# First modulation of a transformer block: column slabs by feature halves, and the first projections in two halves

## The reference, cut to what matters

```python
mod_x = silu(c) @ w_ada + b_ada          # [6 * 1024]; the same for the context with c_ctx
sh1, sc1, gt1, sh2, sc2, gt2 = split(mod_x, 6)
h  = rms_norm(x,   g_attn) * (1 + sc1)  + sh1      # [256, 1024]
hc = rms_norm(ctx, g_attn) * (1 + csc1) + csh1     # [256, 1024]
qa, ka, va, qb, kb, vb = split_projection(h  @ w_qkv)   # widths 512, 128, 128, 512, 512, 512
_,  ka_c, va_c, _, kb_c, vb_c = split_projection(hc @ w_qkv)
# attention, w_o, a mixture of 32 experts, then a retention layer, a gated FFN, an S5 layer, a second FFN
```

## Time and profile before

| | |
|---|---|
| median of the runs | 2076.93 us |
| the profiled execution: its own time | 2072.86 us |
| its span | 2071.0 us |
| TensorE busy | 1957.9 us (95%) |
| VectorE, ScalarE, GpSimd busy | 633.0, 392.8, 201.5 us |
| chain of work that ended last | TensorE 69%, DMA 21%, VectorE 5% |
| loaded from HBM | 613.20 MB, mean 297 GB/s |

### The profile page before, as it was taken

How to read it: one execution, slowest core, us unless ns; L and a number is a source line. 1 busy time by engine, 2 the same in 40 slices (tenths; PEclk the granted TensorE clock), 3 DMA queues, 4 the chain that set the end, 5 groups by cost and what they waited for, 6 DMA issues and landing times.

```text
span 2071.0 us, 24426 instructions
## 1 busy us (share of the span) xinstructions
PE 1957.9 (95%) x9814; PEld 1235.9 (60%) x9814; DVE 633.0 (31%) x1401; ACT 392.8 (19%) x759; POOL 201.5 (10%) x274
## 2 busy tenths in 40 slices
PE   7999999998989998899999899999999999999998
PEld 4645654433333443333334376688888889888887
DVE  3767342213212222112122246331104216210421
ACT  3126211111111101101111021220113215320210
POOL 0000000000000000000000000010755932200000
PEclk9999999999999999999999999999999999999999
DMA  9986699999999999999999995834343342634330
GB/s 372 366 305 246 261 371 416 426 422 428 427 429 428 428 428 428 428 429 428 429 428 428 418 354 206 324 119 142 122 163 123 140 166 99 229 134 150 112 112 21
DMA packets 118928, 615.40 MB, mean 297 GB/s; under 512 B 5216, under 2 KB 9440, under 8 KB 90432
## 3 DMA queue, kind: packets, MB, share of 16 engines
q1 hardware_dynamic: 117088, 604.43, 73.0%
q0 software_dynamic: 1760, 9.83, 1.2%
HBM read 613.20 MB, written 1.05 MB: 297 GB/s over the span
## 4 chain that ended last, share of the span: by engine, by line
PE 69%; DMA 21%; DVE 5%; ACT 2%; issue 1%; SPq 1%; POOL 1%; DVEq 0%; ACTq 0%; POOLq 0%
PE psum L1057 32%; DMA ring<-in_w_in_dram 20%; PE psum L1413 19%; PE psum L1068 3%; PE psum L1377 2%; PE psum L1388 2%; DMA arena<-in_cT_dram 2%; PE psum L1299 1%; PE psum L1562 1%; PE psum L1172 1%; PE psum L1748 1%; PE psum L1104 1%; PE psum L1434 1%; PE psum L1200 1%; SPq L915 1%
## 5 line engine op out<-in xcount | busy, mean ns | idle before, releaser
L1413 PE MATMUL psum<-ring,arena 128*64 128x512 f32 (+1 forms) x3200 | 684.3, 601 | 68.5 <-DMA ring<-in_w_in_dram 67.2
L1057 PE MATMUL psum<-arena,ring 128*128 128x256 f32 (+1 forms) x3072 | 680.4, 384 | 2.1 <-ACT arena L1835 1.4
L1057 PEld LDWEIGHTS psum<-arena,ring 128*128 128x128 f32 x3072 | 581.7, 190 | 99.0 <-issue 18.8
L1413 PEld LDWEIGHTS psum<-ring,arena 128*64 128x64 f32 (+1 forms) x3200 | 222.4, 135 | 504.1 <-issue 434.5
L1968 ACT ACTIVATE arena<-psum 128x512 f32<-128x512 f32 (+1 forms) x144 | 79.0, 571 | 733.6 <-PE psum L1413 726.3
L2548 DVE TENSOR_SCALAR arena<-consts,arena 128x64 f32<-128x64 f32 (+2 forms) x64 | 15.7, 310 | 318.2 <-PE psum L1413 318.2
L2869 DVE SCALAR_TENSOR_TENSOR consts<-psum,smalls,consts 128x255 f32<-128x255 f32 (+1 forms) x88 | 38.4, 478 | 229.8 <-ACT consts L2113 229.0
L2573 DVE TENSOR_TENSOR arena<-psum,arena 128x512 f32<-128x512 f32 x60 | 38.6, 684 | 215.0 <-PE psum L1434 215.0
L2530 DVE SCALAR_TENSOR_TENSOR x<-psum,mod,x 128x256 f32<-128x256 f32 x128 | 55.6, 479 | 145.4 <-PE psum L1388 145.4
L3041 POOL DMA_DIRECT2D arena<-in_pos_dram x1 | 0.5, 543 | 909.0 <-PE psum L1541 909.0
L1388 PE MATMUL psum<-arena 128*128 128x256 f32 (+1 forms) x272 | 69.2, 399 | 3.8 <-issue 2.0
(11 more groups left out here) (397 smaller groups left out, 1656.9 us busy)
## 6 DMA issues: line engine op xcount, KB each, us to landing
ring<-in_w_in_dram SPq DMA_DIRECT2D x124, 2048.0 KB, 17.2
ring<-in_w_out_dram SPq DMA_DIRECT2D x64, 2048.0 KB, 17.2
ring<-in_w_ada_dram SPq DMA_DIRECT2D x36, 2048.0 KB, 13.7
ring<-in_w_up_dram SPq DMA_DIRECT2D x22, 2048.0 KB, 7.9
ring<-in_w_ret_dram SPq DMA_DIRECT2D x12, 2048.0 KB, 16.4
ring<-in_w_down_dram SPq DMA_DIRECT2D x16, 1408.0 KB, 5.9
ring<-in_w_qkv_dram SPq DMA_DIRECT2D x4, 2048.0 KB, 20.0
ring<-in_w_rout_dram SPq DMA_DIRECT2D x4, 2048.0 KB, 9.5
```

The source lines that it names most:

```text
L1057: ins = nc.tensor.matmul(bank(c)[:, at:at + n], w[:, k, m * P:m * P + P], r, start=(k == 0), stop=(k == k_tiles - 1))
L1413: ins = nc.tensor.matmul(psum[at:at + size, p, :], act[:, k, n:n + size], w, start=(k < 3 - halves), stop=(k >= KD - 3 + halves))
```

## The change

The modulation slabs 0 to 3 become column slabs of 512 columns by all 1024 rows, like the others (rows of 2 KB), in the order 0, 2, 1, 3: slab 0 is the shift of tiles 0 to 3, slab 2 their scale, 1 and 3 the same of tiles 4 to 7. The load order is ada0, ada2, qa, (context), kva, ada1, ada3, (small inputs), ada4, ada5, qb, ada6, ada7, kb, (constants), and from there as before. TensorE does half the products of qa, keys and values as soon as tiles 0 to 3 are ready, the other half later, into the same PSUM banks.

```diff
-MOD_KEYS = ([("ada", s) for s in range(12)] + ...
+MOD_KEYS = ([("ada", s) for s in (0, 2, 1, 3, *range(4, 12))] + ...
-GROUP_END = [4, 8, 12, 16, 19, 24, 26, 32, 36]
+GROUP_END = [2, 4, 12, 16, 19, 24, 26, 32, 36]
@@ plan
-    for key in MOD_KEYS[:4]:
+    for key in (*MOD_KEYS[:2], "qa", "kva", *MOD_KEYS[2:4]):
         slab(key, 0)
     chunk(("cols", 0))
-    chunk(("qa", 0), ("norm", 0), ("qa", 1))
-    slabs["qa"] = len(chunks)
+    take_turns(0, 5)
+    chunk(("norm", 0), ("cols", 1))
+    take_turns(2, 3, 1, 0)
+    slab("qa", 2)
     slab("kva", 2)
@@ source
-            if kind == "ada" and s < FIRST_ROWS:
-                return w_ada[T * s:T * s + T, 0:4 * BANK].rearrange("(k p) n -> p k n", p=P)
@@ SyncE
-                if n == 4:
+                if n == 2:
                     sp.dma_start(ctx_x, ...)
@@ TensorE
-            for key in MOD_KEYS[:4]:
+            for key in MOD_KEYS[:2]:
                 modulation_rows(key)
-                keep_busy({1: 6, 2: 6, 3: 1}.get(key[1], 0))
+                keep_busy(6 if key == MOD_KEYS[0] else 2)
             modulation_cols(0)
-            keep_busy(2)
-            (qa with norm(0) inside, keys, values)
+            keep_busy(4)
+            qa_half(0, half_k, 0)          # 16 matmuls of 128x256, tiles 0 to 3
+            norm(0)
+            key_half(1, 0, half_k)         # x tokens, tiles 0 to 3: 4 matmuls of 128x256
+            value_half(1, 0, half_k)       # x tokens: 8 of 128x128
+            modulation_rows(MOD_KEYS[2])   # ada1
+            pe.wait_ge(h_ready, KD)
+            key_half(0, 0, half_k)         # context tokens
+            modulation_rows(MOD_KEYS[3])   # ada3
+            value_half(0, 0, half_k)
+            modulation_cols(1)
+            qa_half(half_k, KD, KD)        # tiles 4 to 7
+            key_half(1, half_k, KD)
+            pe.wait_ge(h_ready, 2 * KD)
+            end(key_half(0, half_k, KD))
+            value_half(1, half_k, KD)
+            end(value_half(0, half_k, KD))
             features("qb", lambda k: h_all[:, k, T:N_KEYS], 2)
@@ ScalarE
-            scale_and_shift(1)
+            scale_and_shift(1, 0, KD // 2)
             norm(0)
             ...
-            scale_and_shift(0)
+            scale_and_shift(0, 0, KD // 2)
+            copy_rows(1)
+            scale_and_shift(1, KD // 2)
+            scale_and_shift(0, KD // 2)
@@ VectorE
-            modulation(0), then aff over 8 tiles (two instructions)
+            first_affine(0)                # bias, then aff of tiles 0 to 3
             add_squares(0)
             norm(0)
+            first_affine(1)                # bias, then aff of tiles 4 to 7
```

More of the change, by code:

```diff
@@ L162 @@
 BIAS_STEP = 13
-MOD_KEYS = ([("ada", s) for s in range(12)] + [("ada2", 0, s) for s in range(12)]
+MOD_KEYS = ([("ada", s) for s in (0, 2, 1, 3, *range(4, 12))] + [("ada2", 0, s) for s in range(12)]
             + [("ada2", 1, s) for s in (0, 1, 2, 3, 4, 5, 10, 11, 6, 7, 8, 9)])
 MOD_NUMBER = {key: n for n, key in enumerate(MOD_KEYS)}
-GROUP_END = [4, 8, 12, 16, 19, 24, 26, 32, 36]
-ROWS_BANK = [4, None, 7, 0, 1, 7, 5, 4, 6]
+GROUP_END = [2, 4, 12, 16, 19, 24, 26, 32, 36]
+ROWS_BANK = [4, 6, 7, 0, 1, 7, 5, 4, 6]
 GAP_KEYS = MOD_KEYS[19:24]
@@ L172 @@
 SUMMED_1 = 8
-FIRST_ROWS = 4
 def group_of(key):
@@ L886, in norm_turn @@
             return NORM_ORDER.index(i)
-        AFFINE = {0: 1, 1: 1, 2: 2, 3: 3, 5: 3, 6: 4, 7: 5}
+        AFFINE = {0: 2, 1: 2, 2: 3, 3: 4, 5: 4, 6: 5, 7: 6}
         def summed_in(n):
@@ L895, in rows_copy @@
         def rows_copy(group):
-            return max(group, 1)
+            return group + 1
         def rows_of(group):
@@ L1092, in modulation_rows @@
                 w = slab(key)
[L1093 to L1100, removed]
                 for k in range(KD):
@@ L1134, in _ @@
             pe.wait_ge(cond_ready, 2)
-            for key in MOD_KEYS[:4]:
+            for key in MOD_KEYS[:2]:
                 modulation_rows(key)
-                keep_busy({1: 6, 2: 6, 3: 1}.get(key[1], 0))
+                keep_busy(6 if key == MOD_KEYS[0] else 2)
             modulation_cols(0)
-            keep_busy(2)
-            features("qa", lambda k: h_all[:, k, T:N_KEYS], 2, first=h_tiles(1), within=lambda: norm(0))
-            pe.wait_ge(h_ready, 16)
-            arrived("kva")
@@ L1144, in _, with room, qa_half @@
-            w = slab("kva")
+            keep_busy(4)
+            def room(key):
+                if USE[key]:
+                    pe.wait_ge(acc_free[BANK_OF[key]], USE[key])
+            def qa_half(k0, k1, first):
+                w = slab("qa")
+                for m in range(4):
+                    for k in range(k0, k1):
+                        if m == 0:
+                            pe.wait_ge(h_ready, first + k - k0 + 1)
+                        ins = nc.tensor.matmul(half(("qa", m // 2), m % 2), w[:, k, m * P:m * P + P],
+                                               h_all[:, k, T:N_KEYS], start=(k == 0 and m % 2 == 0),
+                                               stop=(k == KD - 1 and m % 2 == 1))
+                    if k1 == KD and m % 2:
+                        end(ins)
@@ new lines, in key_half, with value_half @@
+            def key_half(a, k0, k1):
+                w = slab("kva")
+                for k in range(k0, k1):
+                    ins = nc.tensor.matmul(half(("kva", 0), a), w[:, k, 0:P], h_all[:, k, T * a:T * a + T],
+                                           start=(k == 0 and a == 1), stop=(k == KD - 1 and a == 0))
+                return ins
+            def value_half(a, k0, k1):
+                w = slab("kva")
+                for t in (2 * a, 2 * a + 1):
+                    for k in range(k0, k1):
+                        ins = nc.tensor.matmul(bank(("kva", 1))[:, t * P:t * P + P],
+                                               h_all[:, k, t * P:t * P + P], w[:, k, P:2 * P],
+                                               start=(k == 0 and t == 2), stop=(k == KD - 1 and t == 1))
+                return ins
@@ new lines, in _ @@
+            half_k = KD // 2
+            arrived("qa")
+            room(("qa", 0))
+            room(("qa", 1))
+            qa_half(0, half_k, 0)
+            norm(0)
+            arrived("kva")
+            room(("kva", 0))
+            key_half(1, 0, half_k)
+            room(("kva", 1))
+            value_half(1, 0, half_k)
[4 more added lines that the diff above has]
+            value_half(0, 0, half_k)
@@ L1145, in _ @@
+            modulation_cols(1)
+            begin(("qa", 0))
+            begin(("qa", 1))
+            qa_half(half_k, KD, KD)
             begin(("kva", 0))
[L1146 to L1149, removed]
+            key_half(1, half_k, KD)
+            pe.wait_ge(h_ready, 2 * KD)
+            end(key_half(0, half_k, KD))
             begin(("kva", 1))
[L1151 to L1155, removed]
@@ L1156, in _ @@
-            end(ins)
+            value_half(1, half_k, KD)
+            end(value_half(0, half_k, KD))
             features("qb", lambda k: h_all[:, k, T:N_KEYS], 2)
@@ L1827, in apply, with scale_and_shift @@
                 scale_and_shift(i)
-            def scale_and_shift(i):
+            def scale_and_shift(i, k0=0, k1=KD):
                 _, out, row, shift = NORMS[i]
-                act.wait_ge(affine_ready, AFFINE[i])
-                for k in range(KD):
+                act.wait_ge(affine_ready, AFFINE[i] if k1 == KD else 1)
+                for k in range(k0, k1):
                     act.wait_ge(normed_ready, 4 * norm_turn(i) + k // 2 + 1)
@@ L1844, in copy_rows @@
                     act.wait_ge(q_ready, 9)
-                elif group < 6 and group:
+                elif 1 < group < 6:
                     read_ready(act, ("cols", group - 2))
@@ L2268, in modulation @@
                 read_ready(dve, key)
-                at = 16 * (group % 3)
                 if group == 2:
@@ L2274, in modulation @@
                     ins = V.tensor_tensor(out, src, b, ALU.add)
[L2275 to L2279, removed]
+                elif group < 2:
+                    src = bank(key)[:, 0:32].rearrange("p (m n) -> p m n", n=8)[:, :, 0:4]
+                    src = src.rearrange("p m (s c) -> p s m c", c=2)
+                    out = mod[:, 0:16, :].rearrange("p (s h m) c -> p s h m c", s=2, h=2)[:, :, group]
+                    b = sml("b_ada")[:, 0:16].rearrange("p (s h m) -> p s h m", s=2, h=2)[:, :, group]
+                    ins = V.tensor_tensor(out, src, b.unsqueeze(3).to_broadcast([P, 2, 4, 2]), ALU.add)
                 else:
@@ L2294, in _, with first_affine @@
             norm(1)
[L2295 to L2302, removed]
+            def first_affine(group):
+                modulation(group)
+                copied(dve, ("cols", group))
+                dve.wait_ge(dve_step, own.n)
+                tiles, scales = slice(4 * group, 4 * group + 4), slice(8 + 4 * group, 12 + 4 * group)
```

(7 more changed lines are left out.)

## The result

The changed kernel took 2082.63 us (median of 7 runs, 2075.97 to 2085.15) against 2076.43 us for the kernel before (7 runs, 2071.28 to 2077.8). The ratio is 1.0035, with a 95% interval of 1.0023 to 1.0046: about 7.2 us slower (4.8 to 9.6). The profiled execution took 2075.97 us, span 2074.2 us.

What follows compares the result with a forecast made beforehand. Up to 100 us TensorE and the transfer queue were taken to bound the kernel. A 3.3 us later kb start plus 1.5 us of clock fall gave +4.8 us, 2081.7 us against the median; range 2076 to 2085.5.

Steps and rivals of the forecast that it cites:

- Keys and values end at 61.8 (60.9 to 62.4): Early products, set by ada3 landing at 41.2: keys and values end 1.8 us earlier than before (1.2 to 2.7).
- qb is issued when qa is complete and starts 0.9 us after the values: Load of qb waits for qa's slot: issued 54.7, lands 62.7 after 8.0 us from an empty queue.
- Three slabs behind the values instead of one: Before kb, ada6, ada7 and kb must land after the values: 18.8 us instead of 10.2, while qb covers 13.9.
- kb starts at 80.7, +3.3 us: TensorE stalls 4.1 us for kb's slab, so kb starts at 80.7 instead of 77.4; bounds +2.4 to +3.9.
- late by 1.4 us: Before the change, one slab between the rows products of ada2 and ada3 came late for a reason outside its bytes.
- The clock falls, 1.5 us: After TensorE idles about 4 us before kb, the clock drops to the 1.2 GHz level; 0 to 1.7 us, taken 1.5.
- Nothing else behind kb: After kb, vb's slack shrinks to 1.2 us and head norm refinement is 0.4 us late; cost 0, at most 0.4.
- The shift reaches the end whole: Behind vb, loads TensorE needs are issued when it frees slots, so the whole shift was carried to the end.
- Rival C: Not slower: stall absorbed behind kb, in the experts' stream; 0 us, 2076.9 or a little under; chance 0.10.
- Sum: Whole kernel: 3.3 for kb's later start plus 1.5 for the clock, +4.8 us, 2081.7 against the median.
- rival E: A third term: vb's slack gone too or the clock low twice as long; +7 to +8, 2084 to 2085; chance 0.09.
- Rival D (faster): Gain at the values kept, if kb lands by 75.9 or values end at 58.5; 2074 to 2075; chance 0.06.

Runs made afterwards that it cites:

- exchanging the slots: Changed kernel with ring slots of slabs 2 to 5 exchanged, so only kb waits for the values; 2071.29 us against 2073.79 for the kernel before, ratio 0.9985.
- the kernel with coupled slots: Kernel before with only the slot assignment edited, so ada6, ada7 and kb are all issued behind the values; 2081.17 us against 2073.79, ratio 1.0030.
- the kernel kept busy: Changed kernel plus 10 unread matmuls of 128x256 between qb and kb; 2078.81 us against 2073.79 for the kernel before, ratio 1.0019.
- the column slabs alone: Kernel before with column instead of row slabs for ada0 to ada3, in the old order; 2074.13 us against 2073.79, ratio 1.0000.
- The delay alone: Kernel before plus 17 unread matmuls of 128x256 between kb and the head norms; 2082.44 us against 2074.52, ratio 1.0037.

## Why the prediction was right, point by point

- *Keys and values end at 61.8 (60.9 to 62.4).* 62.04 in the profile. ada3 was awaited until 41.72 (41.2 predicted), and the second half of qa began at 47.65 (47.2), behind the 1.2 us for bias, vectors and ScalarE's first tile that the text had there.
- *qb is issued when qa is complete and starts 0.9 us after the values.* Issued at 55.03, started at 62.83, 0.80 us of waiting.
- *Three slabs behind the values instead of one.* Shown in the changed kernel, removed by exchanging the slots, and reproduced in the kernel before.
- *kb starts at 80.7, +3.3 us.* It started at 82.28, +4.9. This term was too small by 1.6 us: from the end of the values to kb's first matmul were 20.2 us, not 18.9. VectorE found ada6 landed at 69.89, as 62.06 + 8.0 would have it, and the two slabs behind it took 12.3 us and not the 10.8 of 2 x 5.42. In the kernel with coupled slots, where kb was awaited just so, they took 10.8 us (71.33 to 82.12):

```profile
69.89 0.48 DVE L2298 TENSOR_SCALAR arena<-ring,cond 128x512 f32<-128x512 f32 x1 [9.32 <-DMA ring<-in_w_ada_dram]
```
```profile
71.33 0.49 DVE L2263 TENSOR_SCALAR arena<-ring,cond 128x512 f32<-128x512 f32 x1 [11.88 <-DMA ring<-in_w_ada_dram]
```

So the 18.8 us that the prediction added up came true there, and what the changed kernel had beyond it is one slab, kb itself, late by 1.2 to 1.5 us in its two profiles and in that of the kernel kept busy. It is of the size of the "late by 1.4 us" between ada2 and ada3, which the prediction left out here. The rate did not fall: from 69.9 to 82.23 us 4.80 MB moved, at 391 GB/s, where two slabs have 4.19, which suggests that bytes of later loads went ahead of kb's last ones. In these three profiles one transfer of the instruction queue lies between the landings of ada7 and kb, and in the coupled kernel none; but with the slots exchanged one lies there too, if only 0.3 us before kb landed, and kb was not late (10.9 us behind ada6). The cause is open.
- *The clock falls, 1.5 us.* It fell, and cost 2.7 (30.29 - 27.5; and 2.7 by the kernel kept busy). Rows 8 had a low stretch of 3.4 us; here the low level held 6.8 us, of which 5.2 lay in kb, so the term was sized from the wrong example. It was also a weaker example than the text took it for. The same gap in front of the last attention products stands in all nine profiles, and a low clock followed it in two, the kernel before and the column slabs alone; the products behind it took 3.62 us in the kernel before and 1.97 in the changed one:

```profile
210.29 3.62 PE L1239 MATMUL psum<-arena 128*128 128x256 f32 x8 [0.78 <-ACT arena L1916]
```
```profile
219.21 1.97 PE L1277 MATMUL psum<-arena 128*128 128x256 f32 x8 [0.78 <-ACT arena L1957]
```

That the fall would come at kb was therefore not shown by that row; the runs show it. The rule of "TensorE: Matmul & The Clock Gate", Part 1, of the Trainium skill, that an idle engine is put at 1.2 GHz, agrees with the fall at 80.6 us and with its absence in the kernel kept busy.
- *Nothing else behind kb.* The +7.6 us of the head norms is found again at the first attention scores (150.2 against 142.6) and, less 0.4, in front of the output projection (221.0 against 213.8).
- *The shift reaches the end whole.* The delay alone shows it to within 2.5 us. Rival C, the stall absorbed down to nothing, is out, by this and by the +7.2 us at the end.
- *Sum.* +4.8 us forecast, +7.2 (4.8 to 9.6) measured. That the time itself came within 0.9 us of the forecast 2081.7 is partly luck: the median of before, from which it was counted, was 0.5 us lower in the seven runs than in the three, and the two medians are only 6.2 us apart. The mechanism was that of the forecast; its two waiting terms were each a third to a half too small, so that the size came out at that of rival E (+7 to +8), whose "low twice as long" is half of what happened.
- *Rival D (faster)* needed the queue to deliver in time; with the slots exchanged it does, and the program is faster.

## What to carry to other kernels

Moving a load forward in a queue whose slots are reused in order also moves its release forward in the list of things that later loads wait for. Before reordering, write down for each later load which use frees its slot, and give the slots that come free late to the loads that are needed late. A stall of some microseconds in front of dense matmuls costs more than its length, as the clock may fall in it: here a start later by 4.9 us became 7.6.

## What was not expected of the hardware

- A wait of 5 us in front of kb gave 6.8 us at the low clock in three of three profiles with that wait (the changed kernel twice, the coupled slots once): kb 30.3, 30.5 and 30.7 us. Where the wait was filled or absent it took 27.5 to 27.7.
- A gap of 1.2 us, with small products before it, was followed by a fall of the clock in one of four profiles with that gap. Two waits of 1.5 to 1.8 and 0.8 us before the output projection were followed by one in two of nine.
- A 2 MB column slab from an empty queue took 8.0 us to land in the kernel before and 7.8 in the changed one (issued 55.03), where one in a full queue follows the last by 5.4 us. Where TensorE waits for that slab, a queue that ran empty costs the difference. Here it ran empty twice: qb was awaited for only 0.80 us after the first time, and the second is in the 20.2 us in front of kb.
